# Modulation computed tile by tile, with the first four in-projections behind it; memory keys and values moved to the second mixer

## The chip, the core and the metric

The kernel runs as one program on one NeuronCore of a Trainium2 chip. The metric is the device time of one execution in microseconds. The program uses five instruction streams: TensorE (PE) for matrix products, VectorE (DVE) and ScalarE (ACT) for elementwise work, GpSimd (POOL) for a few clears and products, and SyncE (SP), whose stream issues every DMA. Each stream runs in its own order; semaphores link them.

## The reference, cut to what matters

One block of a two-mixer network on a batch of 1, 512 tokens of width 1024, in float32. The first mixer is attention beside a convolution, both fed by one modulated norm; the second is an RWKV-style recurrence beside an attention over 256 memory tokens; then a feed-forward layer.

```python
mod = jax.nn.silu(c) @ w_mod[l] + b_mod[l]              # shift, scale, gate: 1024 each
shift, scale, gate = jnp.split(mod, 3, axis=-1)
mod_c = jax.nn.silu(c_ctx) @ w_mod[l] + b_mod[l]        # the same for the context
u = rms_norm(h, norm_w[l]) * (1.0 + scale[:, None, :]) + shift[:, None, :]
uc = rms_norm(hc, norm_w[l]) * (1.0 + scale_c) + shift_c
p = u @ w_in[l]                                         # q, k, v, gates, GLU inputs a and g
k_c, v_c = kv_heads(uc @ w_in[l][:, K_LO:V_HI], k_norm_w[l])
...
u = a * jax.nn.sigmoid(g)                               # then a depthwise convolution, 31 taps
out = jnp.concatenate([attn, conv], axis=-1) @ w_out[l]
h = h + gate[:, None, :] * out
...
log_w = -jax.nn.softplus(-(w0 + jnp.tanh(wd) @ w2)) - 0.5   # low-rank products, rank 64
a = jax.nn.sigmoid(a0 + ad @ a2)
```

The second mixer also norms the 256 memory tokens, multiplies them by a key matrix and a value matrix (1024 to 256 each), and attends to them.

## The kernel before

Activations are feature-major: a tensor of width 1024 is 8 tiles of 128 partitions by 512 tokens. Weights come as blocks of 128 x 1024 values (512 KB), in the order of the list `BLOCKS`, into a ring of 6 slots. The SP stream issues them in that order; a block waits until the last user of its slot is through.

**Split products.** Each large product is made of three passes over float32r parts: `weights_high` (ACT, L1351) copies a block to its high part, `weights_low` (DVE, L1697) makes the low part, the activations have the same two parts, and PE runs three matmuls per tile (L698, L699, L700), 24 per block. Two buffers of high and low weights alternate.

**Front of the program.** SP loads the memory tokens, tables, the small vector table, the context, two key blocks, 8 `shift` and 8 `scale` blocks with the residual `xT` between them, two value blocks, then the in-projection blocks. PE sums the squares of memory and context (L675), makes the memory keys (L685) and their head sums, then the modulation (L727). A modulation block there is 128 rows of the matrix by 1024 columns, so shift and scale are complete only when all 16 blocks are in. PE turns the two rows into columns (L739) and makes the memory values (L766). Meanwhile DVE and ACT norm the memory and the residual; at the end DVE applies scale and shift to the 8 tiles (L1706), ACT makes the high parts (L1357), DVE the low ones (L1702), and the first in-projection `a0` starts (L698).

**In-projections.** 22 blocks: a0 g0 a1 g1 a2 g2 a3 g3, k, v, q0 to q3, zc0 to zc3, za0 to za3. Between them DVE makes gates and convolution taps (L1622; one tap is one instruction of 128x512). `IN_TAPS` says how many taps stand beside each block: 97 of 124 in all. The other 27 (`LATE_TAPS`) are done in attention, `CONV_STEP` = 4 per step.

**Attention.** 16 steps of two heads. In a step PE makes the scores (L854), turns probabilities (L809) and makes values (L873); DVE takes the row maxima (L1808), divides (L1822, L1825) and does its taps; ACT exponentiates (L1388) and copies turned tiles (L1304). The scores of a step wait until the exponentials of the step ahead have freed their banks. Small extra work of PE (gate modulation, convolution statistics, pointwise products) is set by `BESIDE_ATTENTION`.

**Out-projections and second mixer.** PE makes out0 to out7, then the sum of squares `h1_sum` (L708). ACT and DVE norm the residual, split the 8 tiles, and PE makes `wdad` and `gd`, then k_0, the low-rank products w and A of pair 0 (`low_rank`, L708), r_0, v_0, sums, the low-rank products of pair 1, k_1 and r_1. Then 6 pairs of heads follow: for each, an inverse is built in levels 2, 4, 8, 16, 32 (L1006, L1019, L1022, at the last level L1032), solved (L1055), and chained over chunks (L1066 to L1098). `low_rank(p + 2)` stands after the solve of pair p and before a part of the next k projection, whose PSUM bank is the one of w. ACT's exponentials of w and A (L1271) stand behind its two copies of the solution. After the pairs come the mixing and the feed-forward products (from about 750 us on), which the change does not touch.

## Time and profile before

| what | value |
|---|---|
| median of 3 runs | 1159.25 us (1155.62 to 1159.65) |
| the profiled execution, device time | 1152.58 us |
| its span | 1150.8 us |
| TensorE clock granted, mean share of full | 0.987 |
| busy over the span | PE 1070.5 us, DVE 660.6, ACT 431.9, POOL 12.0 |
| moved by DMA | 94.93 MB |

The profile comes from one execution, 6.7 us below the median of the runs. Its span is 1.8 us shorter than its device time. An engine's idle time counts only where another engine waits for it, so the stages are read one by one.

### The profile page before, as it was taken

To read this page: it belongs to the slowest core of one execution; us is meant where nothing else is said; L and a number is where in the kernel's file an instruction comes from. 1 tells how busy PE (TensorE), PEld (TensorE's weight loads), DVE (VectorE), ACT (ScalarE), POOL (GpSimd) and SP (SyncE) were. 2 spreads that over 40 slices of the span, in tenths; PEclk is the share of its full clock that TensorE was granted. 3 is DMA by queue.
4 is the path that set the end of the run, shared out by engine and by line. 5 is a ranking of instruction groups with operands and counts; after the bars stand their busy time and mean duration, and the time that the engine had idled before them with its cause. 6 is when DMAs were issued, how large, how long until landed. Compare 5 with 4: busy or idle time off the path is not lost.

```text
span 1150.8 us, 21841 instructions
## 1 busy us (share of the span) xinstructions
PE 1070.5 (93%) x9476; PEld 820.4 (71%) x9476; DVE 660.6 (57%) x1035; ACT 431.9 (38%) x701; POOL 12.0 (1%) x13
## 2 busy tenths in 40 slices
PE   6799999788997888999998989999999999999998
PEld 4377877465575667777676766678888888888887
DVE  2578899987355576667675826565444222444232
ACT  3333354557533642424333313444443211344121
POOL 0000000000000000000000000000000000000000
PEclk9999999999998989999999999999999999999999
DMA  8841322400032120010110004023222333232330
GB/s 345 319 130 60 104 73 73 148 1 1 19 120 82 51 79 21 21 39 21 39 39 21 21 2 185 3 77 107 92 92 93 109 92 102 87 104 92 110 101 28
DMA packets 25581, 94.93 MB, mean 82 GB/s; under 512 B 2832, under 2 KB 2832, under 8 KB 24976
## 3 DMA queue, kind: packets, MB, share of 16 engines
q1 hardware_dynamic: 25488, 93.54, 24.5%
q8 instruction: 76, 1.25, 0.4%
q14 instruction: 17, 0.14, 0.0%
HBM read 89.34 MB, written 4.19 MB: 81 GB/s over the span
## 4 chain that ended last, share of the span: by engine, by line
PE 57%; DVE 4%; ACT 2%; issue 1%; ACTq 0%; DVEq 0%
PE psum L698 14%; PE psum L699 14%; PE psum L700 14%; PE psum L708 4%; PE psum L1006 2%; PE psum L1019 1%; PE psum L1055 1%; PE psum L974 1%; PE psum L1022 1%; PE psum L1098 1%; PE psum L1089 1%; DVE work L2098 1%; PE psum L996 1%; PE psum L1078 1%; PE psum L928 1%
## 5 line engine op out<-in xcount | busy, mean ns | idle before, releaser
L1697 DVE TENSOR_TENSOR weights_low<-ring,weights_high 128x1024 fp32r<-128x1024 f32 x72 | 88.3, 1226 | 75.0 <-ACT weights_high L1351 75.0
L1351 ACT ACTIVATE weights_high<-ring 128x1024 fp32r<-128x1024 f32 x72 | 75.7, 1052 | 127.5 <-PE psum L700 127.5
L1304 ACT ACTIVATE work<-psum 128x384 f32<-128x384 f32 (+2 forms) x125 | 58.5, 515 | 113.0 <-PE psum L1055 48.9
L698 PE MATMUL psum<-normed_high,weights_high 128*128 128x512 f32 x256 | 100.2, 391 | 0.2 <-DVE weights_low L1697 0.2
L700 PE MATMUL psum<-normed_high,weights_low 128*128 128x512 f32 x256 | 99.7, 390 | 0.0
L699 PE MATMUL psum<-normed_low,weights_high 128*128 128x512 f32 x256 | 99.7, 390 | 0.0
L700 PE MATMUL psum<-hidden_high,weights_low 128*128 128x512 f32 x256 | 99.7, 389 | 0.0
L698 PE MATMUL psum<-hidden_high,weights_high 128*128 128x512 f32 x256 | 99.7, 389 | 0.0
L699 PE MATMUL psum<-hidden_low,weights_high 128*128 128x512 f32 x256 | 99.7, 389 | 0.0
L698 PE MATMUL psum<-pair_normed_high,pair_weights_high 128*128 128x512 f32 x176 | 77.2, 439 | 12.2 <-DVE normed_low L1702 4.2
L1622 DVE SCALAR_TENSOR_TENSOR work<-work,small_sb 128x512 f32<-128x512 f32 x116 | 80.1, 745 | 0.0
L698 PE MATMUL psum<-normed_high,in_weights_high 128*128 128x512 f32 x176 | 70.7, 402 | 2.6 <-DVE in_weights_low L1697 2.6
L699 PE MATMUL psum<-normed_low,pair_weights_high 128*128 128x512 f32 x176 | 70.5, 400 | 0.0
L700 PE MATMUL psum<-pair_normed_high,pair_weights_low 128*128 128x512 f32 x176 | 70.1, 398 | 0.0
L700 PE MATMUL psum<-normed_high,in_weights_low 128*128 128x512 f32 x176 | 68.7, 390 | 0.0
L699 PE MATMUL psum<-normed_low,in_weights_high 128*128 128x512 f32 x176 | 68.5, 389 | 0.0
L1601 ACT ACTIVATE work<-work 128x512 f32<-128x512 f32 x32 | 20.2, 632 | 100.9 <-DVE work L1619 100.9
L698 PEld LDWEIGHTS psum<-normed_high,weights_high 128*128 128x128 f32 x256 | 48.1, 188 | 10.9 <-issue 0.9
L698 PEld LDWEIGHTS psum<-pair_normed_high,pair_weights_high 128*128 128x128 f32 x176 | 33.8, 192 | 30.7 <-issue 10.6
L699 PEld LDWEIGHTS psum<-normed_low,weights_high 128*128 128x128 f32 x256 | 48.1, 188 | 10.1 <-issue 0.2
L698 PEld LDWEIGHTS psum<-hidden_high,weights_high 128*128 128x128 f32 x256 | 48.1, 188 | 10.0
L700 PEld LDWEIGHTS psum<-hidden_high,weights_low 128*128 128x128 f32 x256 | 48.1, 188 | 10.0
(239 smaller groups left out, 2059.0 us busy)
## 6 DMA issues: line engine op xcount, KB each, us to landing
ring<-weights SPq DMA_DIRECT2D x154, 512.0 KB, 3.6
residual<-xT SPq DMA_DIRECT2D x1, 2048.0 KB, 18.6
residual_saved<-residual SPq DMA_DIRECT2D x8, 256.0 KB, 2.0
residual<-residual_saved SPq DMA_DIRECT2D x1, 2048.0 KB, 9.0
outT<-residual SPq DMA_DIRECT2D x8, 256.0 KB, 3.2
work<-memT SPq DMA_DIRECT2D x1, 1024.0 KB, 5.0
work<-ctxT SPq DMA_DIRECT2D x1, 1024.0 KB, 9.9
small_sb<-small SPq DMA_DIRECT2D x1, 907.0 KB, 7.9
```

Source lines behind the costliest of these rows:

```text
L698: pe.matmul(out, wh, high(k), start=first and n == 0, stop=False)
L699: pe.matmul(out, wh, low(k), start=False, stop=False)
L700: ins = pe.matmul(out, wl, high(k), start=False, stop=last and n == len(order) - 1)
L708: full_inc(pe.matmul(take(name, w), stationary, moving, start=True, stop=True), name)
L928: last = pe.matmul(outs["mo"][h * DH:(h + 1) * DH, qt * P:(qt + 1) * P], VMEM[:, t, (2 * j + h) * DH:(2 * j + h + 1) * DH], MPT[:, v % 2, ...
L974: last = pe.transpose(out[:, c, :], src[:, 2 * c:2 * c + 2, :], tab("ident"))
L1006: ins = pe.matmul(out[rows(q), c, :], NT[rows(1 - q), h, c, :], XN[rows(1 - q), h, c, :], start=True, stop=True)
L1304: free_inc(act.activation(out, bank(name, w) if src is None else src, ACT.Copy), name)
L1351: act.activation(WH[group(q)][:, q % 2, :], ring[:, SLOT[b], :], ACT.Copy).then_inc(w_high, 1)
L1601: act.activation(FS[:, t, :], FS[:, t, :], ACT.Square).then_inc(h_relu, 1)
L1622: return vec.scalar_tensor_tensor(out=out, in0=a, scalar=scalar, in1=b, op0=op, op1=ALU.add)
L1697: vec.tensor_tensor(WL[group(q)][:, q % 2, :], ring[:, SLOT[b], :], WH[group(q)][:, q % 2, :].bitcast(F32), ALU.subtract).then_inc(w_low, 1)
```

## The change

It moves work and does not remove any product.

- A shift or scale block is now 128 columns of the matrix with all 1024 rows, so that one block of each gives one tile of 128 features. PE makes a tile `m{k}` with 16 small matmuls of 128 columns (32 records in a trace), on four column groups in turn (`modulated`), ACT copies it, PE turns it (4 columns), and DVE, ACT, DVE make tile k of the residual: product by scale and rstd, high part with the shift as bias, low part.
- Four in-projections (`EARLY` = a0, g0, a1, g1) advance tile by tile in the same loop, each in its own PSUM bank; six weight buffers take the place of two for the first six blocks.
- Nine more places for blocks (15 slots in all) hold the first blocks; residual tiles come first, in four pieces, then two modulation blocks and an in-projection block in turn.
- The context is loaded, summed (at tile 5) and modulated later; its shift is added by ACT.
- The memory's load, norm, keys and values move to the out-projections and to the start of the second mixer. The low-rank weights load later.
- `IN_TAPS` of the first 8 blocks sum to 21 where they were 31; `CONV_STEP` is 5, so 37 taps stand in attention. The convolution's mean is one step later.
- `low_rank(p + 2)` stands before the last level's update, and ACT's two exponentials (`pair_start`) before its copies of the solution.

```diff
-CONV_STEP = 4
+CONV_STEP = 5
-IN_TAPS = [0] + [4, 5] * 3 + [4] + [8, 9, 6, 4, 4, 4, 3] + [4] * 5 + [5, 3]
+IN_TAPS = [0, 2, 0, 3, 4, 3, 5, 4] + [8, 9, 6, 4, 4, 4, 3] + [4] * 5 + [5, 3]
...
+EARLY = ("a0", "g0", "a1", "g1")
+EARLY_BEFORE = {"a0": 0, "g0": 1, "a1": 2, "g1": 3}
+BLOCKS = ([n for k in range(DK)
+           for n in [f"shift{k}", f"scale{k}"] + [x for x in EARLY if EARLY_BEFORE[x] == k]]
+          + IN_BLOCKS[len(EARLY):] + [f"gate{k}" for k in range(DK)] + ["pw0", "pw1"]
...
+EARLY_BLOCKS, EARLY_ROOMS = 2 * DK + len(EARLY), 9
+OWN_BUFFERS = 6
+CTX_TILE = 5
... sync
-            sp.dma_start(MEM, memT).then_inc(mem_in, 16)
-            sp.dma_start(CTX, ctxT).then_inc(ctx_in, 16)
+            for j in range(DK // 2):
+                sp.dma_start(X[:, 2 * j:2 * j + 2, :], xT[:, 2 * j:2 * j + 2, :]).then_inc(x_pair_in[j], 16)
+                if name == "out6":
+                    sp.wait_ge(*is_free(f"pw{CK - 1}"))
+                    sp.wait_ge(*is_free(f"o{NQ - 1}"))
+                    sp.dma_start(MEM, memT).then_inc(mem_in, 16)
+                    sp.wait_ge(out_low, DK)
+                    for i in range(len(MEMORY_BLOCKS)):
+                        sp.dma_start(MEMW[:, i, :], weights[len(BLOCKS) + i]).then_inc(memory_weights_in, 16)
... tensor
+                for kk in range(DK):
+                    for half, wt in enumerate(wts):
+                        group_at = (2 * half + kk % 2) * GROUP_COLS
+                        ins = pe.matmul(out[group_at:group_at + GROUP_COLS, :], SILU_C[:, kk, :],
+                                        wt[:, kk * P:(kk + 1) * P], start=kk < 2, stop=kk >= DK - 2)
+            for k in range(DK):
+                first, second = early_parts(k)
+                pe.wait_ge(u_low, k + 1)
+                early_products(k, first)
+                modulated(k + 2)
+                early_products(k, second)
+                modulated_turn(k + 2)
+                if k == CTX_TILE:
+                    pe.wait_ge(squares, DK // 2 + 1)
+                    sum_over("ctx_sum", lambda k: CTXSQ[:, k, :], DK, SC)
...
+            memory_keys(0, 0, DK // 2)
+            pe.wait_ge(tiles_summed, 1)
             one("h1_sum", tab("ones"), SQ1[:, 0, :])
+            memory_keys(0, DK // 2, DK)
+            memory_keys(1, 0, DK // 2)
...
+            memory_values(0, 5)
             project_part("v_0", 0, DK)
...
             project_part("r_1", 0, DK)
+            memory_values(5, MT * DK)
...
+                    if b == LEVELS[-1] and p + 2 < NP:
+                        low_rank(p + 2)
... scalar
+            for k in range(DK):
+                act.wait_ge(x_scaled, k + 1)
+                act.activation(UH[:, k, :], U[:, k, :], ACT.Identity, bias=MOD[:, 0, k, 0:1]).then_inc(u_high, 1)
+                if k < len(EARLY) - 1:
+                    weights_high(k + 1)
+                modulated_rows(k + 2)
+                if k == CTX_TILE - 1:
+                    act.wait_ge(ctx_in, 16)
+                    act.activation(CTXSQ, CTX, ACT.Square).then_inc(squares, 1)
+                if k == CTX_TILE:
+                    rms("ctx_sum", RS[:, 1, 0:SC], SC, 1.0 / D, EPS, rstd)
... vector
+            for k in range(DK):
+                modulated_columns(k)
+                scaled_product(U[:, k, :], X[:, k, :], MOD[:, 1, k, 0:1], RS[:, 0, :]).then_inc(x_scaled, 1)
+                if k < len(EARLY):
+                    weights_low(k)
+                if k == DK - 1:
+                    context_scaled(0, 2)
+                vec.wait_ge(u_high, k + 1)
+                vec.scalar_tensor_tensor(out=UL[:, k, :], in0=U[:, k, :], scalar=MOD[:, 0, k, 0:1],
+                                         in1=UH[:, k, :].bitcast(F32), op0=ALU.add, op1=ALU.subtract).then_inc(u_low, 1)
```

PE's stream at the front of the program, before:

```order
1 L675 MATMUL psum<-work,tables_sb 128x256 x16
2 L685 MATMUL psum<-work,ring 128x256 x16
3 L708 MATMUL psum<-head_squares,tables_sb 128x256 x2
4 L727 MATMUL psum<-ring,silu_cols 32x512 x16
5 L708 MATMUL psum<-work,tables_sb 128x512
6 L727 MATMUL psum<-ring,silu_cols 32x512 x16
7 L739 MATMUL psum<-tables_sb,t_t_61 128x4 x4
8 L739 MATMUL psum<-tables_sb,work 128x4 x4
9 L766 MATMUL psum<-ring,work 128x256 x16
10 L698 MATMUL psum<-normed_high,in_weights_high 128x512
```

and now (L822 is the modulation, L777 its turn, L767 to L769 the three passes of a split product):

```order
1 L744 MATMUL psum<-work,tables_sb 128x512 x4
2 L822 MATMUL psum<-work,silu_cols 32x128 x16
3 L777 MATMUL psum<-tables_sb,t_t_61 128x4
4 L822 MATMUL psum<-work,silu_cols 32x128 x16
5 L777 MATMUL psum<-tables_sb,t_t_61 128x4
6 L767 MATMUL psum<-normed_high,in_weights_high 128x512
```

The first pass of a0 stands behind two modulation tiles, where it stood behind all of the modulation and the memory's products.

ACT's stream now, in the tile loop from tile 4 on (L1428 copies a modulation tile, L1474 makes the high part of a tile, L1480 squares the context, L1380 and L1382 make its rstd; before, the eight high parts stood in one row):

```order
21 L1428 ACTIVATE t_t_61<-psum 128x128
22 L1474 ACTIVATE normed_high<-normed,mod_cols 128x512
23 L1428 ACTIVATE t_t_61<-psum 128x128
24 L1480 ACTIVATE work<-work 128x2048
25 L1474 ACTIVATE normed_high<-normed,mod_cols 128x512
26 L1428 ACTIVATE t_t_61<-psum 128x128
27 L1380 ACTIVATE rstd<-psum 128x256
28 L1382 ACTIVATE rstd<-rstd 128x256
29 L1474 ACTIVATE normed_high<-normed,mod_cols 128x512 x2
```

The high part of tile 5 stands behind the squares of the context, and that of tile 6 behind the context's rstd, which waits for PE.

PE's stream at the end of a pair (pair 1), before:

```order
L1006 MATMUL psum<-work 64x64 x16
L1032 MATMUL psum<-work 64x64 x16
L1055 MATMUL psum<-work 64x128 x16
L708 MATMUL psum<-work,small_sb 128x512 x2
L698 MATMUL psum<-pair_normed_high,pair_weights_high 128x512
```

and now:

```order
L1127 MATMUL psum<-work 64x64 x16
L777 MATMUL psum<-work,small_sb 128x512 x2
L1153 MATMUL psum<-work 64x64 x16
L1176 MATMUL psum<-work 64x128 x16
L767 MATMUL psum<-pair_normed_high,pair_weights_high 128x512
```

The two low-rank products stand ahead of the last update and the solve, no longer between the solve and the projection.

## Rows read from the trace of the kernel before

**Rows 1.** Page, section 1: busy time, share of the span, instructions of each engine.

```profile
PE 1070.5 (93%) x9476; PEld 820.4 (71%) x9476; DVE 660.6 (57%) x1035; ACT 431.9 (38%) x701; POOL 12.0 (1%) x13
```

**Rows 2.** Windows: length, busy us of each engine, then granted clock, DMA share, GB/s.

```profile
0.00:25.00 25.00, 15.87 (x64) 13.15 (x65) 7.12 (x23) 7.40 (x11) 2.36 (x6) 1.00 0.93 374
25.00:50.00 25.00, 17.70 (x82) 4.19 (x80) 10.72 (x17) 8.45 (x17) 0.00 (x0) 0.93 0.88 330
60.00:110.00 50.00, 49.53 (x219) 41.09 (x220) 40.38 (x62) 17.51 (x24) 0.00 (x0) 1.00 0.31 101
110.00:198.00 88.00, 87.18 (x385) 69.11 (x383) 77.59 (x114) 38.38 (x59) 0.00 (x0) 1.00 0.26 84
198.00:242.00 44.00, 33.94 (x268) 20.27 (x266) 41.88 (x69) 24.49 (x54) 0.00 (x0) 0.96 0.29 96
242.00:283.00 41.00, 36.76 (x310) 24.22 (x310) 28.60 (x50) 28.48 (x60) 0.00 (x0) 1.00 0.01 1
```

**Rows 3.** Timeline of PE at the front: start, duration, instruction, idle and releaser.

```profile
50.71 7.15 PE L766 MATMUL psum<-ring,work 128*128 128x256 f32 x32
...
60.47 0.47 PE L698 MATMUL psum<-normed_high,in_weights_high 128*128 128x512 f32 x1 [2.61 <-DVE in_weights_low L1697]
```

**Rows 4.** Timeline: the first load's arrival; modulation blocks as they land.

```profile
5.77 1.91 ACT L1308 ACTIVATE work<-work 128x2048 f32<-128x2048 f32 x1 [3.76 <-DMA work<-memT]
...
46.11 0.19 PEld L727 LDWEIGHTS psum<-ring,silu_cols 128*32 128x32 f32 x4 [1.15 <-DMA ring<-weights]
47.39 0.19 PEld L727 LDWEIGHTS psum<-ring,silu_cols 128*32 128x32 f32 x4 [1.09 <-DMA ring<-weights]
```

**Rows 5.** Timeline of ACT and DVE: squares, split parts of a tile, low weights.

```profile
12.01 1.91 ACT L1310 ACTIVATE work<-work 128x2048 f32<-128x2048 f32 x1 [4.33 <-DMA work<-ctxT]
...
55.22 0.68 DVE L1702 TENSOR_TENSOR normed_low<-normed,normed_high 128x512 fp32r<-128x512 f32 x1
55.33 0.63 ACT L1357 ACTIVATE normed_high<-normed 128x512 fp32r<-128x512 f32 x1 [0.70 <-DVE normed L1706]
```

**Rows 6.** Timeline of PE: matmuls of several shapes at full clock.

```profile
109.54 3.62 PE L685 MATMUL psum<-work,ring 128*128 128x256 f32 x16
...
121.71 3.73 PE L789 MATMUL psum<-ring,work 128*128 128x128 f32 x32
...
218.55 1.53 PE L873 MATMUL psum<-work 128*64 128x128 f32 x24
...
220.81 1.06 PE L727 MATMUL psum<-ring,silu_cols 128*32 128x512 f32 x8
221.89 1.56 PE L854 MATMUL psum<-work 64*128 64x512 f32 x8
```

**Rows 7.** Timeline of DVE in attention: taps of a step, row maxima.

```profile
216.24 2.73 DVE L1622 SCALAR_TENSOR_TENSOR work<-work,small_sb 128x512 f32<-128x512 f32 x4
218.89 1.82 DVE L1808 TENSOR_REDUCE small_temps<-psum 128x1 f32<-128x768 f32 x2
...
247.90 1.82 DVE L1808 TENSOR_REDUCE small_temps<-psum 128x1 f32<-128x768 f32 x2 [2.65 <-PE psum L854]
```

**Rows 8.** Timeline of PE and DVE from the out-projections to pair 0.

```profile
365.70 1.89 PE L708 MATMUL psum<-work,tables_sb 128*128 128x512 f32 x2 [2.24 <-DVE work L1642]
...
400.51 0.47 PE L698 MATMUL psum<-pair_normed_high,pair_weights_high 128*128 128x512 f32 x1 [2.37 <-DVE pair_weights_low L1697]
...
424.81 2.07 PE L708 MATMUL psum<-head_squares,tables_sb 128*128 128x512 f32 x2 [4.69 <-ACT head_squares L1506]
...
419.17 0.43 DVE L1629 TENSOR_SCALAR sigmoids<-sigmoids 128x512 f32<-128x512 f32 x1 [1.94 <-ACT sigmoids L1271]
```

**Rows 9.** Timeline of PE at the end of pair 1.

```profile
505.64 1.15 PE L1032 MATMUL psum<-work 64*64 64x64 f32 x32 [0.75 <-DVE work L2063]
506.94 1.97 PE L1055 MATMUL psum<-work 64*64 64x128 f32 x32 [0.15 <-issue]
508.83 1.13 PE L708 MATMUL psum<-work,small_sb 64*128 64x512 f32 x4
510.81 0.50 PE L698 MATMUL psum<-pair_normed_high,pair_weights_high 128*128 128x512 f32 x1 [0.85 <-ACT sigmoids L1271]
```

396 lines of the change are left out of this document (237 added, 159 removed).

## The prediction

> **What bounds the kernel now.** I read the busy line first: PE is busy for 93% of the span [rows 1], so a gain must come from stretches in which PE waits, or from a better overlap of them. The windows show where these are [rows 2]. In the first 50 us PE is busy 33.6 us while the DMA engines run at 93% and 88%: the front waits for loads. From 60 to 198 us PE has next to no idle time. From 198 to 242 us DVE is busy 41.9 of 44 us and PE 33.9: attention is bound by DVE there. From 242 to 283 us DVE falls to 28.6 of 41 us. Later, PE waits in single gaps: before h1_sum, v_0 and the key sum of pair 1 [rows 8], and at the end of a pair [rows 9].
>
> The front ends when a0 starts, at 60.47 us; nine in-projection blocks later it is 109.54 us [rows 3, 6], so a block takes 5.45 us and g1, the fourth, is through at 60.47 + 21.8 = 82.3 us. The first point of comparison is when g1 is through in the changed kernel.
>
> **The front.** Loads: a block of 512 KB lands every 1.28 us [rows 4]. The first load, two blocks long, was there at 5.77 us [rows 4], so a load that ends after n blocks lands at 3.2 + 1.28 n us. Now the residual is first (4 blocks, and 0.4 for the two small tables): it is there at 8.8 us. The modulation pairs, with the in-projection blocks between them, land at 11.4, 15.2, 19.0, 22.8, 26.7, 29.2, 34.3 (behind the context) and 36.9 us.
>
> PE's work per tile: an m tile is 32 records of 128 columns. Modulation matmuls of 512 columns ran four at a time, 8 in 1.06 us [rows 6], which is 0.033 us for each 128 columns; 24 records of 128 columns on two column groups took 1.53 us, 0.064 each; 32 on the whole array took 3.73 us, 0.117 each [rows 6]. I take 1.0 us for a tile, near the first since the column groups are used alike; the ends are 0.9 and 3.7 us. The turn takes 0.3 us with its waits. A tile of one in-projection is 5.45/8 = 0.68 us. All tile products together are 4 x 5.45 = 21.8 us, as before.
>
> The first tiles go at the pace of a chain: residual in, squares and pair sums (1.0 + 0.7), the sum on PE (two low-clock matmuls took 1.89 us [rows 8], so about 12.5 us for its end), rstd 1.3, m0 and its copy and turn, product 0.7, high part 0.63, low part 0.68 [rows 5]. ACT handles the row copy of tile k+2 ahead of the high part of tile k+1, so tiles 0, 1, 2 are ready at about 18, 22 and 25 us. From tile 2 on PE is full. Tile 2: 1.36 + 1.0 + 2.05 + 0.3 = 4.7 us, until 30. Tile 3: 2.05 + 1.0 + 2.7 + 0.3 = 6.1, until 36. Tiles 4 and 5: 2.05 + 1.0 + 0.7 + 0.3 = 4.05 each. Two waits come in that the order shows: the high part of tile 5 stands behind the row copy and the context's squares (1.91 us, [rows 5]), which costs PE 2.6 us; the high part of tile 6 stands behind the context's rstd, which waits for ctx_sum (8 matmuls, 3.62 us, [rows 6]), 2.2 us more. Then 36 + 4.05 + 2.6 + 4.05 + 3.6 + 2.2 + 2 x 2.7 = 57.9 us. For the clock I add 1.0: it stood at 0.93 of full from 25 to 50 us in the trace of before [rows 2], and the new front has PE idle in pieces as well. **g1 is through at 59 us, 23.3 us earlier.** With m at 3.7 us it would be about 72; with no stall at all 53.
>
> What hides the rest: the memory's products were 3.62 x 2 (keys) and 7.15 us (values, [rows 3]) in the front; they are now later and are priced there.
>
> An m tile switches PE between a four-group and a whole-array form. The trace shows the switch: after 8 four-group matmuls the next one starts when they have ended, at 221.89 for 221.87 us [rows 6], while two forms on the whole array elsewhere overlap by some 0.17 us. The Trainium skill ("TensorEngine Tiling (Array Packing)", Key Properties) says that changing the tiling mode drains TensorE; by that rule 12 switches in the loop from tile 2 on cost some 2 us, estimated from that overlap, and the trace agrees. The 1.0 us of a tile has room for it.
>
> **In-projections after g1.** PE's 18 blocks and the small products took 82.3 to 198.2 us, 116 us, nearly without idle time [rows 2]. DVE's own work in the same stretch now: 87 taps at 0.67 us (four take 2.73 with their overlap, [rows 7]) = 58 us, 16 weights_low at 1.15 = 18, 24 gate operations of 0.4 to 0.6 = 12, rotary 14, waits for rstd and ACT 6: 108 us, under 116. One place is late: the first gates, taps and the context's shift all come after g1, and ACT copies the weights of a3 only after eight context tiles. I put 1 us on PE there. So attention starts 22.3 us earlier.
>
> **Attention.** Each of the seven first steps gets a fifth tap, 0.665 us, in a stretch where DVE is the bound. Late taps go from 27 to 37: 6.7 us of DVE. DVE had a wait of 2.65 us in step 8 [rows 7], which takes the last of them, so 4 to 5 us are left. The later mean only moves 1.88 us of PE from step 7 to step 9, and both statistics steps of the variance into one. **+4.5 us**, ends 0 (PE catches up in the PE-bound steps) and +6.7.
>
> **Second mixer up to pair 0.** Memory adds PE work: keys 7.2, values 7.2, mem_sum and head sums 1.5 us, together 16 us. Its cover: the gaps of 2.24 us, of the norm (wdad is paced by DVE there, about 1.3 us a tile against 0.68 us of PE), of 2.37 and of 4.69 us [rows 8]. Key products in the first gap and between the tiles of wdad fit; h1_sum no longer runs at 1.2 GHz, as it did after 2.24 us of idle time (1.89 us for two records that take 1.13 elsewhere). Until r_0 the two kernels are level. memory_values(0, 5) takes 2.3 us in a gap of 2.37, the other eleven 5.0 us in one of 4.69. ACT's early exponentials (pair_start) save the two waits of DVE for them (one of 1.94 us, [rows 8]) and bring pair 1's inputs forward by about 2 us; and with no gap the key sum takes 1.1 us and not 2.07. **-2.6 us.** Ends: -5 (all of the low clock comes back) and +3 (values delay the key sum and DVE does not gain).
>
> If the cover were gone, the 16 us would stand on the path. SP waits for o3 and pw3, then for all low parts of the gated tiles, before it loads out6: memory (2 blocks) and four blocks land by about 332 us on the old axis, out6 one block after, 15 us before its use. mem_norm on DVE delays out6's addition by about 1 us beside PE's out7: nothing.
>
> **Pairs.** In pairs 1 to 3 PE waits 0.75 us before the last update (for DVE's masks), then 0.85 us before the projection, for the bank that ACT frees by its exponential of w, 1.1 us of it behind the low-rank products [rows 9]. The low-rank products (about 1.0 us) move into the first gap, so the update is 0.3 us later, and the projection follows the solve at once: 0.96 - 0.3 + 0.85, about 1.5 us each; in pair 0, without the first gap, 1.0. Pairs 4 and 5 have none. **-5.5 us**, ends -6.5 and 0 (the solve is the longer chain through DVE and ACT, and copies come later).
>
> **Sum.** -22.3 + 4.5 - 2.6 - 5.5 = -25.9. From the profiled execution, 1152.6, this gives 1126.7; the runs' median is 6.7 us above that execution, and from 1159.25 it gives 1133.3. I forecast **1133 us**.
>
> **Rivals.**
> 1. *The small modulation matmuls do not overlap.* At 0.064 to 0.117 us a record a tile takes 2.0 to 3.7 us, and PE is the bound in the loop: g1 at 64 to 72. For it: half of the records I have for 128 columns run so. Against: the same column groups at 512 columns ran four at a time. Sum: 1138 to 1147. Chance 0.2.
> 2. *The load order gives all, but DVE gives it back.* The first five steps of DVE's in-projection loop start late, taps run behind to the end and attention's steps take the whole 6.7 us, and the values stand in the path: 1133 + 3 (taps) + 2 + 3 = 1141. For it: only 8 us of slack in 116. Chance 0.12.
> 3. *It goes better.* No stall at the context's squares or rstd, attention absorbs half of the taps, the pairs give 6.5: 1133 - 5 - 2 - 3 = 1123, or a little less. Chance 0.1.
> 4. *Slower than before.* The clock gate: small matmuls and waits leave PE at 1.2 GHz through the whole tile loop. PE's 33 us of work between 18 and 58 us then take 66, g1 is through at about 91, 9 us later than before, and with +4.5 - 2.6 - 5.5 the time is about 1165 (less than 6 us over). It decides from some 17 us of loop work at half clock on, at which the front gains only the 6 us that attention takes. Against: before, PE was busy only 17.7 of 25 us from 25 to 50 and the mean clock was 0.93. Chance 0.03.
> 5. *It doesn't do what it says.* Loads issued without waits share the engines and the first residual pieces come late, near 30 us; the loop then starts 12 us later: 1145. Against: in the trace of before, ten loads were on the way and the first was in at 5.8 us. Chance 0.05.
>
> **How the numbers follow.** The forecast's own band, 1126 to 1140, has 0.5. The range of 1120 to 1147 holds it, rivals 1 and 2 and most of 3 and 5. Within 0.5% (5.8 us, about what a measurement of this kernel can tell from no change) would need 20 us of the 26 to be lost: 0.04; slower by more than that 0.04; faster 0.92.
>
> **What would show it.** In the changed profile: the first split product near 18 us; g1's gate exponential near 59; PE gaps of about 2 us at tiles 5 and 6; modulation groups of 32 records in 1.0 us; attention steps of 6.3 us at first, where they were 5.6; no gap over 1 us before v_0 and the key sum of pair 1, and a clock of 1.0 there; no wait for the exponential of w in the pairs. If the records of L822 stand 0.1 us apart, or DVE is over 95% busy from 60 to 175 us, the sum is wrong.

## The result

The changed kernel took 1145.83 us (median of 4 runs, 1142.65 to 1147.52), the kernel before beside it 1159.45 us (1155.62 to 1163.23). The ratio is 0.9888, 95% interval 0.9865 to 0.9912: **faster by 1.1%, 13 us**. In a second comparison, on the chip of the first experiments, the ratio was 0.9861 (0.9838 to 0.9885): 1140.56 for 1158.05 us. The forecast was 1133 us, 26 us below; the measured time lies in its range, but the gain is half to two thirds of what was forecast.

### The profile page after: what moved, and what is told of

Same layout as the page of the kernel before. It is cut to its first block, busy times and chain, and to the rows that moved or that the text cites. A ratio compares the mean times of both kernels' runs of the same rounds, so it can differ in the third digit from the quotient of the medians.

```text
span 1142.5 us, 22265 instructions
## 1 busy us (share of the span) xinstructions
PE 1071.6 (94%) x9660; PEld 825.2 (72%) x9660; DVE 658.2 (58%) x1032; ACT 435.6 (38%) x711; POOL 12.1 (1%) x13
## 3 DMA queue, kind: packets, MB, share of 16 engines
q1 hardware_dynamic: 26064, 93.54, 24.2%
## 4 chain that ended last, share of the span: by engine, by line
PE 81%; DVE 10%; ACT 4%; issue 3%; DMA 1%; SPq 0%; ACTq 0%; DVEq 0%
PE psum L767 20%; PE psum L768 19%; PE psum L769 19%; PE psum L777 5%; PE psum L1127 3%; PE psum L927 2%; DVE work L1773 2%; DVE small_temps L1952 1%; PE psum L898 1%; PE psum L943 1%; PE psum L1140 1%; PE psum L1176 1%; PE psum L1095 1%; PE psum L1199 1%; DMA work<-weights 1%
## 5 line engine op out<-in xcount | busy, mean ns | idle before, releaser
L1458 ACT ACTIVATE weights_high<-ring 128x1024 fp32r<-128x1024 f32 x72 | 75.7, 1052 | 127.5 <-PE psum L769 127.5
L767 PE MATMUL psum<-normed_high,weights_high 128*128 128x512 f32 x256 | 100.1, 391 | 0.2 <-DVE weights_low L1829 0.2
L769 PE MATMUL psum<-normed_high,weights_low 128*128 128x512 f32 x256 | 99.6, 389 | 0.0
L767 PE MATMUL psum<-hidden_high,weights_high 128*128 128x512 f32 x256 | 99.6, 389 | 0.0
L769 PE MATMUL psum<-hidden_high,weights_low 128*128 128x512 f32 x256 | 99.6, 389 | 0.0
L1428 ACT ACTIVATE work<-psum 128x384 f32<-128x384 f32 (+2 forms) x124 | 58.1, 514 | 72.3 <-PE psum L898 29.9
L767 PE MATMUL psum<-pair_normed_high,pair_weights_high 128*128 128x512 f32 x176 | 77.0, 438 | 3.0 <-DVE work L1770 2.2
L769 PE MATMUL psum<-pair_normed_high,pair_weights_low 128*128 128x512 f32 x176 | 69.4, 394 | 0.0
L767 PE MATMUL psum<-normed_high,in_weights_high 128*128 128x512 f32 x144 | 60.1, 417 | 7.9 <-DVE normed_low L1859 6.9
L769 PE MATMUL psum<-normed_high,in_weights_low 128*128 128x512 f32 x144 | 57.1, 397 | 0.0
L768 PE MATMUL psum<-normed_low,in_weights_high 128*128 128x512 f32 x144 | 56.9, 395 | 0.0
L767 PEld LDWEIGHTS psum<-normed_high,weights_high 128*128 128x128 f32 x256 | 48.0, 188 | 10.9 <-issue 0.9
L767 PEld LDWEIGHTS psum<-hidden_high,weights_high 128*128 128x128 f32 x256 | 48.0, 188 | 10.1
L769 PEld LDWEIGHTS psum<-normed_high,weights_low 128*128 128x128 f32 x256 | 48.0, 188 | 10.0
L769 PEld LDWEIGHTS psum<-hidden_high,weights_low 128*128 128x128 f32 x256 | 48.0, 188 | 10.0
```

Of the source, the lines that this page charges most:

```text
L767: pe.matmul(out, wh, high(k), start=first and n == 0, stop=False)
L768: pe.matmul(out, wh, low(k), start=False, stop=False)
L769: ins = pe.matmul(out, wl, high(k), start=False, stop=last and n == len(order) - 1)
L1428: free_inc(act.activation(out, bank(name, w) if src is None else src, ACT.Copy), name)
L1458: act.activation(wsplit(q)[0], room_of(b), ACT.Copy).then_inc(w_high, 1)
```

## Profile after

The busy line answers to [rows 1]: the busy times of PE and DVE are the same within 3 us, so the gain is idle time of PE that went.

```profile
PE 1071.6 (94%) x9660; PEld 825.2 (72%) x9660; DVE 658.2 (58%) x1032; ACT 435.6 (38%) x711; POOL 12.1 (1%) x13
```

The windows answer to [rows 2] (length, busy us, granted clock, DMA share, GB/s). The changed kernel is about 14 us ahead in the third and fourth, so they hold other work than before.

```profile
0.00:25.00 25.00, 12.58 (x113) 7.04 (x113) 9.00 (x21) 11.31 (x18) 0.51 (x5) 0.89 0.93 351
25.00:50.00 25.00, 21.47 (x195) 16.20 (x196) 10.67 (x22) 7.15 (x11) 0.00 (x0) 0.91 1.01 409
60.00:110.00 50.00, 46.95 (x210) 37.76 (x210) 40.91 (x63) 23.35 (x38) 0.92 (x1) 1.00 0.17 53
110.00:198.00 88.00, 83.19 (x355) 61.67 (x353) 76.29 (x112) 36.89 (x57) 0.00 (x0) 0.94 0.28 90
198.00:242.00 44.00, 34.61 (x300) 23.49 (x302) 43.69 (x72) 24.60 (x56) 0.00 (x0) 0.96 0.22 73
242.00:283.00 41.00, 34.92 (x287) 22.70 (x284) 29.60 (x53) 29.75 (x63) 0.00 (x0) 1.00 0.00 1
```

The front is still full of loads (0.93 and 1.01 of the DMA engines), the clock is at 0.89 and 0.91 there, and from 198 to 242 us DVE has 0.3 us of idle time: attention's first steps are bound by DVE more than before.

PE's timeline, with idle time and releaser in brackets, in answer to [rows 3, 8, 9]:

```profile
14.09 1.08 PE L822 MATMUL psum<-work,silu_cols 128*32 128x128 f32 x32
...
17.37 1.08 PE L822 MATMUL psum<-work,silu_cols 128*32 128x128 f32 x32 [1.31 <-DMA work<-weights]
...
20.29 0.80 PE L767 MATMUL psum<-normed_high,in_weights_high 128*128 128x512 f32 x1 [1.01 <-DVE normed_low L1859]
...
25.74 0.79 PE L767 MATMUL psum<-normed_high,in_weights_high 128*128 128x512 f32 x1 [0.81 <-DVE normed_low L1859]
...
31.19 0.50 PE L767 MATMUL psum<-normed_high,in_weights_high 128*128 128x512 f32 x1
...
49.50 0.50 PE L767 MATMUL psum<-normed_high,in_weights_high 128*128 128x512 f32 x1 [2.71 <-DVE normed_low L1859]
...
61.27 0.50 PE L767 MATMUL psum<-normed_high,in_weights_high 128*128 128x512 f32 x1 [2.32 <-DVE normed_low L1859]
...
79.34 0.47 PE L767 MATMUL psum<-normed_high,in_weights_high 128*128 128x512 f32 x1 [1.02 <-DVE in_weights_low L1829]
...
187.73 1.23 PE L943 MATMUL psum<-work 64*128 64x512 f32 x2 [3.29 <-DVE work L1946]
...
423.12 1.10 PE L777 MATMUL psum<-head_squares,tables_sb 128*128 128x512 f32 x2 [0.78 <-ACT memory_keys_values L1428]
...
502.26 1.96 PE L1176 MATMUL psum<-work 64*64 64x128 f32 x32 [0.16 <-issue]
504.16 0.50 PE L767 MATMUL psum<-pair_normed_high,pair_weights_high 128*128 128x512 f32 x1
```

And a step of attention on DVE, in answer to [rows 7]:

```profile
212.58 3.40 DVE L1773 SCALAR_TENSOR_TENSOR work<-work,small_sb 128x512 f32<-128x512 f32 x5
215.90 1.82 DVE L1952 TENSOR_REDUCE small_temps<-psum 128x1 f32<-128x768 f32 x2
217.63 0.16 DVE L1966 RECIPROCAL small_temps<-small_temps 128x2 f32<-128x2 f32 x1
217.82 1.15 DVE L1969 TENSOR_SCALAR normed<-normed,small_temps 128x768 f32<-128x768 f32 x2
218.88 3.40 DVE L1773 SCALAR_TENSOR_TENSOR work<-work,small_sb 128x512 f32<-128x512 f32 x5
```

The first rows are modulation tiles, 32 records in 1.08 us, the second of which waits 1.31 us for its load. Tiles 0, 1 and 2 start at 20.3, 25.7 and 31.2 us. The steps of 5.45 us between them fall into 10.2 us in which PE was granted 1.2 GHz. The gaps at tiles 5 and 6 (2.71 and 2.32) and before a3 (1.02) are those that were forecast. The 3.29 us before the first scores were not. In pair 1 the projection at 504.16 follows the solve at once, where it waited 0.85 us. A step of attention is 6.3 us of DVE (212.58 to 218.88) without idle time.

The points at which the stages end, read in the traces (us). The two middle columns are a second profiled execution of each kernel, from the experiments:

| | before | before_again | after_again | after |
|---|---|---|---|---|
| g1's last product | 82.5 | 84.7 | 66.9 | 67.1 |
| last in-projection | 198.3 | 200.5 | 184.3 | 184.4 |
| out0 starts | 319.7 | 323.2 | 315.0 | 315.2 |
| out7 ends | 363.5 | 368.5 | 360.9 | 361.1 |
| pair 0's first products | 426.8 | 432.8 | 424.0 | 424.1 |
| pair 4's first products | 636.5 | 642.7 | 628.9 | 627.8 |
| last instruction | 1150.8 | 1156.8 | 1143.4 | 1142.5 |

From the first and the last column, stage by stage: front -15.4, in-projections +1.5, attention +9.3, out-projections +2.1, up to pair 0 -0.2, pairs 0 to 3 -6.1, rest +0.5: together -8.3 us. The forecast had -23.3, +1, +4.5, nothing, -2.6 and -5.5. Between the second pair of executions, before_again and after_again, the stages differ by -17.8, +1.6, +8.0, +0.5, -1.1, -5.2 and +0.4, together -13.4 us. So the front and attention are to be explained, and besides why the profiles differ by 8 us and the medians by 13 to 17.

Part of that is which executions were profiled. The experiments below give more executions of the same code in these two stages. In the table (us) "low" is the time in the stage in which PE was granted 1.2 GHz. low_rank_back, no_memory, filled_front and ctx have the changed kernel's attention as it is; low_rank_back and no_memory also its front, and 'banks' both but for the PSUM banks.

| execution | its time, median of its kernel | low up to g1 | g1 through | low in attention | attention to out0 |
|---|---|---|---|---|---|
| before | 1152.6, 1159.3 | 3.4 | 82.5 | 6.8 | 121.4 |
| before_again | 1158.6, 1157.8 | 13.7 | 84.7 | 6.8 | 122.7 |
| after | 1144.3, 1145.8 | 13.6 | 67.1 | 17.1 | 130.7 |
| after_again | 1145.2, 1140.6 | 13.6 | 66.9 | 17.1 | 130.7 |
| low_rank_back | 1153.1, 1142.4 | 10.3 | 65.4 | 10.2 | 127.4 |
| no_memory | 1135.4, 1137.7 | 6.8 | 64.6 | 10.3 | 127.4 |
| filled_front | 1138.7, 1138.4 | 3.4 | 65.7 | 10.2 | 127.5 |
| ctx | 1138.6, 1143.3 | 3.4 | 56.6 | 13.6 | 127.2 |
| banks | 1138.9, 1140.6 | 3.4 | 64.8 | 10.2 | 126.5 |

Two things follow. Where before and changed front had about the same low time, the front gained 17.6 or 17.7 us (84.7 to 67.1 with 13.7 and 13.6; 82.5 to 64.8 with 3.4, by the front of 'banks'), not 15.4. And the two profiles of the changed kernel have more low clock in attention than the others: the same attention code took 127.2 to 127.5 us four times. A stage that is compared with after_again, whose profiled run is the longest of its six, looks better by about 2 us in the front and 3 us in attention by the clock alone.

## Experiments

All medians, with the ratio to the kernel before and its interval:

| kernel | median us | ratio | 95% interval |
|---|---|---|---|
| after_again | 1140.56 | 0.9861 | 0.9838 to 0.9885 |
| banks | 1140.63 | 0.9853 | 0.9829 to 0.9877 |
| taps | 1142.88 | 0.9879 | 0.9857 to 0.9900 |
| ctx | 1143.25 | 0.9880 | 0.9851 to 0.9909 |
| early_split | 1141.45 | 0.9861 | 0.9838 to 0.9883 |
| low_rank_back | 1142.40 | 0.9882 | 0.9849 to 0.9915 |
| no_memory | 1137.72 | 0.9836 | 0.9811 to 0.9861 |
| filled_front | 1138.40 | 0.9835 | 0.9813 to 0.9857 |
| reordered | 1133.40 | 0.9784 | 0.9753 to 0.9815 |
| reordered_filled | 1131.55 | 0.9769 | 0.9747 to 0.9791 |
| reordered_taps | 1129.61 | 0.9757 | 0.9735 to 0.9778 |
| reordered_92 | 1128.25 | 0.9753 | 0.9718 to 0.9788 |
| before_banks | 1159.57 | 1.0019 | 1.0002 to 1.0036 |
| low_rank_on_pe | 1157.82 | 1.0010 | 0.9991 to 1.0030 |
| low_rank_alone | 1153.89 | 0.9973 | 0.9949 to 0.9997 |
| before_again | 1157.82 | 1.0006 | 0.9979 to 1.0033 |

The kernels ran on four chips: after_again, banks, taps and ctx on one; early_split, low_rank_back, no_memory and filled_front on a second; the four from 'reordered' to reordered_taps and before_banks on a third, the rest on a fourth; across chips the ratios compare, not the times. Differences of 1 to 3 us between kernels are within these intervals; for them the stages in the traces are read, but each trace is one execution, and a difference of 1 to 3 us of a stage can be its clock.

### The two kernels again

No edit.

> The changed kernel as it is, run beside the experiments that change one thing in it, so that their differences are read on one chip. Expected: 1143 to 1148 us (1145.8 before), front through g1 at 67.1 us, last in-projection over at 184.4, a 3.3 us gap of PE before the first scores, out0 at 315.

> The kernel before as it is, for a second profiled execution, since the first was faster than its runs' median. Expected of theory E (the executions of one kernel differ only in where PE runs at half clock): span 1150 to 1158 us, the same waits of PE at the same places, and the difference of the spans within 1 us of half of the difference of the times at low clock in which PE is busy.

The cores' rows (span, mean granted clock) of before, before_again, after and after_again:

```profile
core 0: 1150.8 us, clock 0.987
```
```profile
core 0: 1156.8 us, clock 0.981
```
```profile
core 0: 1142.5 us, clock 0.983
```
```profile
core 0: 1143.4 us, clock 0.982
```

The median of after_again, 1140.56 us, is below the 1143 to 1148 us that were expected. The in-projections after g1 take 115.8 us in both executions of before, to 0.01 us. They differ where PE was granted 1.2 GHz: 30.7 us of the first span, 44.4 us of the second. Half of the 13.7 us between them is 6.8, the spans differ by 6.0. So theory E stands in the time, within its 1 us; the waits of PE are nearly the same behind a0, but not in the front, where the second execution has one more wait for a load (1.65 us) and 3.13 us before a0 for 2.61. Of the 11 runs of before beside after_again none was over 0.985; the lowest clock, 0.976, belongs to the longest time, 1161.6, and the two highest, 0.984 and 0.985, to the two shortest, 1153.6 and 1153.9. Of the 64 runs of before beside all experiments three reached 0.988 (1150.6, 1153.8 and 1154.1 us). The first profiled execution, 0.987, was therefore an unusually quick one of this kernel, while the changed kernel's 0.983 lies in the lower half of its own ten runs (0.979 to 0.989). Against before_again the changed kernel's spans are 13.4 and 14.3 us shorter, which is what the medians say.

### Attention: banks, before_banks, taps

**banks** swaps the PSUM banks of the front:

```diff
-            o.append((f"m{k}", 1, 4 + k % 2))
+            o.append((f"m{k}", 1, k % 2))
...
-            o.append((f"mt{k}", 1, 6 + k % 2))
+            o.append((f"mt{k}", 1, 2 + k % 2))
...
-            o.extend((x, 1, EARLY.index(x)) for x in early_parts(k)[late] if EARLY_BEFORE[x] == k)
+            o.extend((x, 1, 4 + EARLY.index(x)) for x in early_parts(k)[late] if EARLY_BEFORE[x] == k)
...
-    o.extend((x, 1, 4 + n) for n, x in enumerate(IN_BLOCKS[len(EARLY):2 * CK]))
+    o.extend((x, 1, n) for n, x in enumerate(IN_BLOCKS[len(EARLY):2 * CK]))
```

> One thing: the PSUM banks of the front are swapped (early projections in banks 4 to 7, the modulation's tiles in 0 to 3), so that the banks that rotate through the in-projections end as they did in the kernel before: za0 to za3 in banks 4 to 7, the first scores' banks 0 to 3 free. Theory B (the bank of za3 holds the first scores back): the gap of 3.3 us before the scores goes, the first scores start within 0.3 us of the end of the last in-projection, PE is not throttled from 186 to 197 us, out0 comes 4 to 6 us earlier and the time is 1140 to 1142. Rival (attention is bound by DVE with its fifth tap, the wait only shows it): DVE's steps run as before, out0 comes less than 1.5 us earlier, and the time is 1144 to 1146.

**before_banks** brings the same assignment of banks into the kernel before:

```diff
-    add("kx", "kc", "hs2", "rot0", "hs3", "vx", "v_lo")
+    o.append(("kx", 1, 0))
+    add("kc", "hs2", "rot0", "hs3", "vx", "v_lo")
```

> The kernel before, with one thing changed: the rotation of the PSUM banks starts four later at the keys, so that za0 to za3 end in banks 0 to 3, where the first scores need them free, as they do in the changed kernel. Theory B: the first scores, which start 0.1 us after the last in-projection in the kernel before, wait for DVE's gate of za3, 3.3 us, the first steps of attention run at the low clock, and attention to out0 takes 124 to 127 us in place of 121.4; time 1160 to 1163 for 1158. Rival (the wait is only a sign of DVE's lag in the changed kernel): a gap of less than 1.5 us, out0 within 1 us of before.

The first scores on PE, in the kernel before and then in before_banks:

```profile
197.91 0.39 PE L700 MATMUL psum<-normed_high,in_weights_low 128*128 128x512 f32 x1
198.23 1.56 PE L854 MATMUL psum<-work 64*128 64x512 f32 x8
```
```profile
201.71 1.22 PE L855 MATMUL psum<-work 64*128 64x512 f32 x2 [3.29 <-DVE work L1803]
```

The same 3.29 us appear to 0.01 us in the other kernel, by nothing but banks. All seven profiled executions with the changed kernel's banks have it, and none of the ten with other banks. From the last in-projection to out0 before_banks takes 124.4 us for 121.4 and 122.7 in the two executions of before, and its ratio is just above 1. In 'banks' the wait is gone, the scores start with the last in-projection's end, and this stage takes 126.5 us. That is 4.2 us less than in after_again, but only 0.9 to 1.0 less than in low_rank_back, no_memory and filled_front, which have the wait and the same 10.2 us of low clock. So theory B holds for the wait; what the wait costs is about 1 us here and 1.7 to 3.0 us in the kernel before, and in the medians 'banks' and after_again are the same. The other 3.3 us of the 4.2 are 6.9 us more of low clock, which varies from 10.2 to 20.5 us between executions that all have the wait. The mechanism: the banks rotate with each small product. The change takes small products out of the front and pins others, so that za0 to za3 ended in banks 0 to 3, where the scores of step 0 need four free banks, and za3's is freed last, by its gate on DVE (L1946), after its sigmoid on ACT. The Trainium skill ("Perfetto Trace Analysis", Matmuls) says that groups should rotate through different banks so that emptying one overlaps the next group's matmuls; the rows agree, and add that a pinned stage behind a rotation needs the rotation to end on the other banks.

**taps** puts the numbers of before into the changed kernel:

```diff
-CONV_STEP = 5
+CONV_STEP = 4
-IN_TAPS = [0, 2, 0, 3, 4, 3, 5, 4] + [8, 9, 6, 4, 4, 4, 3] + [4] * 5 + [5, 3]
+IN_TAPS = [0] + [4, 5] * 3 + [4] + [8, 9, 6, 4, 4, 4, 3] + [4] * 5 + [5, 3]
```

> One thing: the taps as in the kernel before (31 in the first eight blocks, 27 late, four a step). Prediction's theory (taps cost DVE 4.5 us in attention): attention from the last in-projection to out0 gets 4 to 5 us shorter (126 for 130.7), but the 10 taps, 6.7 us, now stand in the in-projections, where DVE had about 8 us of slack: they cost 0 to 3 us there; time 1141 to 1145. Rival (attention's extra 9 us are the bank wait and the low clock, not taps): attention gets less than 1.5 us shorter and the time is 1145 to 1148.

Windows, from g1's end to the last in-projection and from there to out0, of before, after and taps:

```profile
82.50:198.30 115.80, 114.98 (x509) 91.97 (x507) 101.96 (x147) 49.19 (x73) 0.00 (x0) 1.00 0.25 78
198.30:319.70 121.40, 102.56 (x794) 64.28 (x793) 88.00 (x146) 73.09 (x156) 0.00 (x0) 0.97 0.14 44
```
```profile
67.10:184.40 117.30, 115.52 (x507) 91.75 (x505) 101.33 (x148) 52.59 (x82) 0.00 (x0) 1.00 0.25 79
184.40:315.20 130.80, 106.56 (x794) 66.12 (x793) 94.92 (x156) 73.45 (x156) 0.00 (x0) 0.93 0.12 41
```
```profile
65.00:188.50 123.50, 117.07 (x507) 92.86 (x505) 108.32 (x159) 52.34 (x82) 0.00 (x0) 0.97 0.23 76
188.50:313.40 124.90, 107.42 (x792) 66.75 (x792) 88.00 (x146) 73.00 (x156) 0.00 (x0) 0.92 0.13 42
```

Ten taps are 6.9 us of DVE (94.92 - 88.00), as forecast. In 'taps' attention gets 5.8 us shorter and the in-projections 6.2 us longer, where 0 to 3 were expected: a3 waits 5.66 us for its weights, and the low clock follows. The prediction's theory holds for attention; DVE's slack in the in-projections is not where the early taps stand. So the extra 9.3 us of attention are about 5 for taps ('banks' against before, with 3.4 us more of low clock), about 1 for the bank and about 3 for the clock of these two executions; in the four others attention was 5.8 to 6.1 us longer than in the first execution of before.

### The front: ctx, filled_front, early_split, reordered

**ctx** puts the context's squares, sum and rstd behind tile 7:

```diff
-                if name == f"shift{CTX_TILE + 1}":
+                if name == "shift6":
...
-CTX_TILE = 5
+CTX_TILE = DK - 1
...
-                if k == DK - 1:
-                    context_scaled(0, 2)
```

> One thing: the context's squares, its sum and rstd stand after tile 7 and not at tiles 4 and 5 (its load stays where it is). Theory F (ACT's in-order context work makes PE wait at tiles 5 and 6, 2.7 + 2.3 us, and the stall is what drops the clock at 50 us): both gaps go, PE keeps the high clock through 60 us, g1 is through at 60 to 62 us in place of 67.1; ctx_sum stays 1 us behind it, g3 is 3 to 5 us earlier; time 1140 to 1143. Rival (the chain through DVE and ACT paces tiles 4 to 7 anyway): g1 at 65 to 67, time 1144 to 1147.

g1 is through at 56.6 us, 10.3 earlier. Of this 3.6 are the context's sum, which now stands behind g1, and 2.1 are there at tile 2, ahead of both gaps, by the clock; each gap shrank to 0.9 us. But the last in-projection ends at 183.2, only 1.1 earlier, and the median did not fall (1143.25 us, above the expected 1140 to 1143). PE's row behind g1:

```profile
63.30 0.47 PE L767 MATMUL psum<-normed_high,early_high 128*128 128x512 f32 x1 [3.22 <-DVE early_low L1829]
```

PE does the context's sum (3.6 us) and then waits 3.22 us for a2's weights and 1.77 for a3's, which ACT and DVE split behind the context's work; some of the clock is lost with it. Neither expectation had this: the wait that was removed was replaced by one behind it.

**filled_front** adds matmuls without use:

```diff
+            def filler(n):
+                for _ in range(2 * n):
+                    pe.matmul(bank("g1", P), tab("ones"), tab("ones"), start=True, stop=True)
...
                 modulated(k)
+                filler(2 - k)
                 modulated_turn(k)
+                filler(4 - k)
```

and four more behind m2 and its turn each.

> Added: 26 matmuls of 128 columns on the table of ones, into a bank that is overwritten later, in the gaps of PE beside the first three modulation tiles (15 to 25 us). Their results are not used. Theory K (the idle time of PE from 15 to 20 us brings the low granted clock of 19 to 29 us): the clock stays at 1.0 from 16 to 45 us, g1 is through at 63 to 65 us in place of 66.9, time 1138 to 1140. Rival (the first tiles are paced by the chain through DMA, ACT and DVE, so that the clock costs nothing there): g1 moves by less than 1 us, and the filling itself may cost up to 1 us; 1140 to 1142.

These are 28 matmuls (56 records), not 26. Windows of 15 to 30 us in after_again and in filled_front, and the starts of tiles 1 and 2 there:

```profile
15.00:30.00 15.00, 10.39 (x112) 7.21 (x113) 7.95 (x14) 5.70 (x11) 0.00 (x0) 0.66 1.03 417
```
```profile
15.00:30.00 15.00, 14.77 (x205) 12.68 (x195) 8.93 (x17) 7.69 (x13) 0.00 (x0) 1.00 1.03 417
...
25.89 0.48 PE L767 MATMUL psum<-normed_high,in_weights_high 128*128 128x512 f32 x1
...
29.79 0.50 PE L767 MATMUL psum<-normed_high,in_weights_high 128*128 128x512 f32 x1 [0.23 <-DVE normed_low L1870]
```

With PE kept busy the clock stays at 1.00 where it was 0.66; tile 0 starts 1.9 us later, at 22.0, tile 2 1.2 us earlier, g1 at 65.7 for 66.9, where 63 to 65 were expected. A step from tile to tile takes 3.90 us here, with ACT's order unchanged, and 5.45 us in the changed kernel's low stretch; 'taps' and 'ctx', whose low stretch ends at 23.6 us, have 3.91 from tile 1 to 2. The median is 2 us lower, inside the intervals; its clock in four of five runs is 0.991 or more, which no run of after_again and two of six of low_rank_back, on the same chip, reached. Theory K stands for the clock; that the filling is worth time is not shown: with the same front and without it g1 was through at 64.6, 65.0 and 65.4 us in no_memory, 'taps' and low_rank_back.

**early_split** is banks and ctx together, and splits the weights of a2 and g2 inside the loop:

```diff
+                if k in (5, 6):
+                    weights_high(k - 1)
...
-            weights_high(4)
-            weights_high(5)
...
+                if k in (6, 7):
+                    weights_low(k - 2)
...
-            weights_low(4)
-            context_scaled(2, DK)
-            weights_low(5)
+            context_scaled(0, DK)
```

> Three things together: the banks swapped as in 'banks', the context's squares and sum behind tile 7 as in 'ctx', and the weights of a2 and g2 split by ACT and DVE inside the tile loop (tiles 5 to 7) and the context's scaling after them. Theory (behind the loop PE waits for the split weights of a2 and a3, 3.2 and 1.8 us in 'ctx', and nothing else stands between g1 and attention but PE's own 116 us): g1 through at 56 to 59 us, no gap over 1.5 us before a3's products are over, the last in-projection is over at 175 to 178 us (184.4 in the changed kernel, 183.2 in 'ctx'), out0 at 302 to 305, time 1132 to 1135. Rival (DVE bounds the whole of the front and the in-projections, 101 us of work in 117 with the taps in order): the gain comes back as waits at later blocks, last in-projection at 181 to 183, time 1138 to 1141.

A miss: 187.1 us at the last in-projection, later than the changed kernel, and 1141.45 us. PE and ACT:

```profile
79.08 0.77 PE L767 MATMUL psum<-normed_high,in_weights_high 128*128 128x512 f32 x1 [3.54 <-DVE in_weights_low L1829]
```
```profile
73.44 3.29 ACT L1495 ACTIVATE work<-work,mod_cols 128x256 f32<-128x256 f32 x8
76.64 1.99 ACT L1458 ACTIVATE in_weights_high<-ring 128x1024 fp32r<-128x1024 f32 x2
```

a3's high part stands behind the eight context tiles on ACT. PE waits 3.54 us, and runs at the low clock from 78.3 to 85.2 us. It is not DVE's load that gives the gain back (102.9 of 126.2 us), it is one item of ACT's order.

**reordered** mends this one and the first tiles:

```diff
+                if k:
+                    modulated_rows(k + 1)
                 if k < len(EARLY) - 1:
                     weights_high(k + 1)
-                modulated_rows(k + 2)
...
+                    weights_high(6)
                     rms("ctx_sum", RS[:, 1, 0:SC], SC, 1.0 / D, EPS, rstd)
...
-                if x == "g1":
+                if x == "g2":
...
-            context_scaled(0, DK)
+            weights_low(6)
```

(the row copy now stands behind the next tile's high part and ahead of the weights; the context's scaling moves to a2's turn on DVE).

> 'early_split' with two more moves on ACT and DVE: the high part of tile k + 1 stands before the row copy of tile k + 2 on ACT, and a3's weights are split before the context's rstd, its scaling and shift, which follow behind g2's gate. Theory P1 (tile k + 1 waits for the product of tile k and the modulation of tile k + 2 through ACT's order, 5.4 us a tile): tile 1 starts at 23 to 24 us (25.6 before), tile 2 at 27 to 28.5 (31.0), g1 is through at 57 to 59. Theory P2 (a3's weights behind the context's work cost 3.5 us and the low clock that follows them another 3.4): no gap over 1.5 us before a3, no low clock from 70 to 90 us, last in-projection over at 176 to 179 (187.1 in 'early_split', 184.3 in the changed kernel), time 1132 to 1135. Rival (DVE is too full, the waits move to later blocks): 181 to 184 and 1138 to 1141.

ACT's order beside the first tiles, in after and then in reordered:

```profile
18.57 0.28 ACT L1428 ACTIVATE t_t<-psum 128x128 f32<-128x128 f32 x1 [2.00 <-PE psum L822]
18.74 0.71 ACT L1474 ACTIVATE normed_high<-normed,mod_cols 128x512 fp32r<-128x512 f32 x1
19.35 1.04 ACT L1458 ACTIVATE in_weights_high<-memory_keys_values 128x1024 fp32r<-128x1024 f32 x1
24.02 0.28 ACT L1428 ACTIVATE t_t<-psum 128x128 f32<-128x128 f32 x1 [3.62 <-PE psum L822]
24.19 0.71 ACT L1474 ACTIVATE normed_high<-normed,mod_cols 128x512 fp32r<-128x512 f32 x1
```
```profile
18.46 0.71 ACT L1474 ACTIVATE normed_high<-normed,mod_cols 128x512 fp32r<-128x512 f32 x1
19.07 1.04 ACT L1458 ACTIVATE in_weights_high<-memory_keys_values 128x1024 fp32r<-128x1024 f32 x1
21.04 0.72 ACT L1474 ACTIVATE normed_high<-normed,mod_cols 128x512 fp32r<-128x512 f32 x1 [0.93 <-DVE normed L1772]
23.61 0.28 ACT L1428 ACTIVATE t_t<-psum 128x128 f32<-128x128 f32 x1 [1.85 <-PE psum L822]
```

In after tile 1's high part waits 3.62 us behind the row copy of m2, which waits for PE; in reordered it is made at 21.04. Tiles 1 and 2 start at 24.2 and 27.7 us, g1 is through at 54.2, a3 waits 0.61 us, the last in-projection ends at 174.6 and out0 starts at 301.2. Both theories hold, and the median is 7 us below after_again's (ratio 0.9784 for 0.9861). Not all of tile 2's 3.3 us is the order: 'ctx', with ACT's old order and the same 3.4 us of low clock, starts tile 2 at 28.95, and has g1 through at 56.6. So the order is worth 1.2 us at tile 2 and 2.4 at g1. With the clock high throughout (reordered_filled) the step from tile 1 to 2 is 3.51 us for 3.90.

### Slack of DVE: reordered_filled, reordered_taps, reordered_92

These add the filler to 'reordered' (reordered_filled), and then move ten taps (reordered_taps) or five (reordered_92) out of attention:

```diff
-CONV_STEP = 5
-IN_TAPS = [0, 2, 0, 3, 4, 3, 5, 4] + [8, 9, 6, 4, 4, 4, 3] + [4] * 5 + [5, 3]
+CONV_STEP = 4
+IN_TAPS = [0, 2, 0, 2, 3, 4, 5, 5] + [8, 9, 7, 5, 5, 5, 4] + [5] * 5 + [5, 3]
```
```diff
-CONV_STEP = 5
-IN_TAPS = [0, 2, 0, 3, 4, 3, 5, 4] + [8, 9, 6, 4, 4, 4, 3] + [4] * 5 + [5, 3]
+CONV_STEP = 4
+IN_TAPS = [0, 2, 0, 3, 4, 3, 5, 4] + [8, 9, 8, 5, 5, 4, 4] + [4] * 5 + [5, 3]
```

> 'reordered' with the 26 matmuls of 'filled_front' in PE's first gaps. Theory K (the idle time brings the low clock): no low clock before 45 us; the first tiles are up to 1.5 us later by the filling itself, g1 within 1.5 us of 'reordered'; time 0 to 3 us below 'reordered', 1131 to 1134. Rival (the low clock there hides behind the chain): the same time or 1 us more.

> 'reordered_filled' with ten taps moved from attention's first steps (four a step, 27 late) into the in-projections, all of them from g3's block on (33, 40... 97 in place of 87 there). Theory D (DVE has 16 us of slack in the 117 us of the in-projections once a3 is passed, none in attention's first steps): in-projections as long as in 'reordered_filled' within 1 us, attention 4.5 to 6 us shorter (121 to 122.5 in place of 126.5), time 1126 to 1130. Rival (the ten taps cost in the in-projections what they give in attention, as in 'taps', where 6.2 us came for 5.7): the same time as 'reordered_filled' within 2 us.

> 'reordered_filled' with five taps moved from attention into the keys', values' and queries' blocks, four a step, none more in the last eight blocks. In 'reordered_taps' the five more in the last blocks made DVE late for PE at the end of the in-projections (waits of 1.3 us at 149.7 and 4.4 us before the second scores). Theory D2 (these five were the harm): no wait at 149, the scores wait 1.7 us as in 'reordered_filled', attention 122.5 to 124.5 us, out0 at 299 to 301, 1127 to 1129 us. Rival (DVE has no slack for any): as 'reordered_taps', 1129 to 1131.

PE's gaps in reordered_taps, and in reordered_92:

```profile
183.35 1.08 PE L796 MATMUL psum<-ring,silu_cols 128*32 128x512 f32 x4 [4.38 <-DVE work L1959]
```
```profile
149.66 0.47 PE L767 MATMUL psum<-normed_high,in_weights_high 128*128 128x512 f32 x1 [1.16 <-DVE in_weights_low L1842]
...
180.34 0.64 PE L796 MATMUL psum<-ring,silu_cols 128*32 128x512 f32 x4 [1.71 <-DVE work L1959]
```

In reordered_filled the clock is high from 15 us until 180, and g1 is through at 55.7 for 54.2 us; between theory K and its rival the medians, 1131.55 and 1133.40, don't decide. The five more taps in the last blocks made DVE late: 4.38 us before the gate's modulation for 1.71, as D2 says; but the wait at 149.7 us stays with five taps too (1.16 for 1.32), where D2 expected none. In-projections and attention are 120.4 + 127.5 us in reordered_filled, 121.4 + 125.0 in reordered_taps, 121.8 + 124.3 in reordered_92. So moving five to ten taps gives 1.5 to 2 us, not 4.5 to 6, and less if the clock is counted: the trace of reordered_filled has 17.1 us of low clock in attention, those of the other two and of 'reordered' 13.7, and 'reordered', without the move, takes 120.4 + 126.5. The medians fell by 1.9 us (reordered_taps beside reordered_filled, one chip). **reordered_92 is the fastest kernel of this study, 1128.25 us**, 2.5% below the kernel before; between it and the two ahead of it the intervals overlap, and its ratio, 0.9753, is that of reordered_taps, 0.9757.

### Memory and low rank: no_memory, low_rank_back, low_rank_on_pe, low_rank_alone

**no_memory** leaves out products two to seven of every eight of the memory's keys and values:

```diff
                 for k in range(lo, hi):
+                    if 0 < k < DK - 1:
+                        continue
```

> Of the memory's key and value products only the first and last of each group of eight are made, so the memory's keys and values are not computed in full; all else stands. It takes away about 11 us of PE's work between out7 and the key sum of pair 1. Theory (the products lie in waits that are there anyway): r_0 and the key sum of pair 1 come less than 1.5 us earlier and the time is 1139 to 1141. Rival (they stand on the path, and this is why the start of the second mixer gained nothing net): the key sum of pair 1 comes 3 to 8 us earlier and the time is 1133 to 1138.

From wdad's start to gd's end PE takes 15.16 us with them left out and 15.15 with them: key products beside wdad cost nothing. From out0 to pair 0's first products it is 108.2 for 109.0 us, though 2.1 us at low clock fell in it there; the key sum of pair 1 comes 1.7 us earlier. The median is 3 us lower, in the range of the rival, and its interval overlaps that of after_again. So most of the 11 us of products is hidden, as forecast, and about 2 us of it are not.

**low_rank_back** undoes the low-rank part:

```diff
-                    if b == LEVELS[-1] and p + 2 < NP:
-                        low_rank(p + 2)
...
                     solve(p, h)
+                if p + 2 < NP:
+                    low_rank(p + 2)
```

and ACT's `pair_start(p + 2)` stands behind the copies of wu again; **low_rank_on_pe** and **low_rank_alone** bring into the kernel before the reverse edit, on PE alone and on both engines.

> One thing undone: the low-rank products of pair p + 2 and ACT's first exponentials stand behind the solve again. The prediction's theory (1.5 us in each of pairs 1 to 3, 1.0 in pair 0): a pair takes 51.9 us from first level to first level instead of 51.2, the first level of pair 4 stands 4 to 5.5 us later than in the changed kernel, measured from the start of pair 0, and the time is 1144 to 1147 beside 1140.6. Rival (the solve is then late by other waits, the move gives nothing): less than 1.5 us, 1140 to 1142.

> The kernel before with one part of the change alone: the low-rank products of pair p + 2 stand before the last level's update on PE; ACT's exponentials stay where they were. The prediction's theory: the bank wait before the projection stays in part, since ACT reads the banks late; a pair gains 0.5 to 1.0 us in pairs 0 to 3. Rival: the banks' wait was behind ACT all the time, so nothing is gained, or the products delay the update by 1.0 us each: 0 to -0.3 us a pair, pair 0 to pair 4 209 to 211 us (209.7 before).

> The kernel before with the low-rank part of the change whole: the products before the last update on PE, and ACT's first exponentials of pair p + 2 ahead of the copies of wu. The prediction's theory: 1.5 us in each of pairs 1 to 3 and 1.0 in pair 0, pair 0 to pair 4 in 204 us (209.7 before), 1152 to 1153 beside 1157.7. By 'low_rank_back', which lost 2.9 us of the changed kernel's 6.1, it is rather 2.5 to 3.5 us: 206 to 207 and 1154 to 1156, and the rest of the 6.1 is pair 0, which no longer starts at the low clock.

From pair 0's to pair 4's first products: 209.7 us in before, 210.0 in before_again, 211.0 with the move on PE alone, 208.6 with both (206.9 without half of the 3.4 us at low clock that fell in it), 206.3 in low_rank_back, 203.7 and 204.9 (with 3.4 us at low clock) in the changed kernel. The move on PE alone gives nothing: the projection waits 1.27 us for ACT in place of 0.85. With ACT's exponentials the wait goes (its median is 0.3% below before, the interval just under 1), and undoing both costs the changed kernel 1.5 to 2.7 us, between the theory's 4 to 5.5 and the rival's less than 1.5. Its 6.1 us are therefore only in part the low-rank move. Pair 0 is 1.8 us shorter in low_rank_back too (49.98 for 51.82), and there the kernel before starts it at the low clock, behind the 4.69 us gap of [rows 8]. Pair 3 is 2.2 us shorter in it (51.93 for 54.15): two gaps of PE with no releaser are gone, of which the first is, in before and in before_again,

```profile
604.29 0.21 PE L1022 MATMUL psum<-work 64*64 64x64 f32 x1 [1.46 <-issue]
```
```profile
610.21 0.21 PE L1022 MATMUL psum<-work 64*64 64x64 f32 x1 [1.43 <-issue]
```

## Why the prediction was half right

The direction, the stages and most waits were right. The step that failed is the front, -23.3 us forecast and -15.4 measured in the first pair of profiles, -17.6 at equal low clock: the chain of the first tiles with its clock term. Attention's missing term for the bank and the varying clock, and the start of the second mixer, make up the rest.

- **A modulation tile**: 1.0 us forecast, 1.08 measured. Right; rival 1 falls. Where the clock was low, a tile took 1.94 us. At high clock it starts 0.07 us before the modelled end of the product ahead, and the next product 0.07 us before its own end (33.80 for 33.87 us), where products in a row overlap by 0.16; so the 12 switches of form cost about 1 us by the prediction's own measure (an estimate), not some 2.
- **The chain of the first tiles**: tiles 0, 1, 2 at "about 18, 22 and 25 us" were 20.3, 25.7, 31.2. Of the 8.1 us that g1 was late against the forecast of 59, 6.2 are there at tile 2. The first 2.3 are tile 0: the residual's sum ended at 14.2 us, not 12.5, and ACT's copy of m1's row stands ahead of tile 0's high part (18.57, then 18.74 us), with a load that released PE at 17.37 us where 15.2 was forecast. About 0.8 are the period. The prediction names its cause, the row copy of tile k + 2 ahead of the high part of tile k + 1, which closes a loop through PE (product, modulation, copy, high part, low part), and prices it at 3 to 4 us: that is nearly right at the high clock (3.90 in filled_front). The other 3.1 are two turns of this loop at 1.2 GHz (5.45 each).
- **The clock**: +1.0 forecast. From 19.3 to 29.5 and from 50.0 to 53.4 us PE ran at 1.2 GHz. The first stretch cost the 3.1 us, the second 1.5 (from tile 5 to 6 11.77 us, for 10.27 in 'banks', which had no low clock there), so the term was 4.6 us in this execution. In others it was less: g1 was through at 64.6 to 65.7 us. The term was undersized, and it varies. The last 1.5 us of the 8.1 are 0.2 to 0.5 us by which each step from tile 2 on is longer than priced.
- **Tiles 5 and 6**: 2.6 and 2.2 forecast, 2.71 and 2.32 measured. Right in place and size; that removing them brings almost nothing, because of a3's weights and the context's work behind them, was not seen. "No stall at all, 53" would have been true only with ACT's order changed too.
- **In-projections after g1**: +1 forecast, +1.5, with the 1.02 us gap at a3. Right; DVE's work there was 101.3 us, not 108.
- **Attention**: the taps' term, +4.5, was right (+5.1 in 'banks'). Two terms were not in the sum: the bank of the first scores, a wait of 3.29 us worth about 1 us of the stage, and the clock, about 3 us more in the two profiled executions of the changed kernel than in the others. The order and the plan of the banks were there to be read before; the prediction followed engines and loads across the moved instructions, not the banks.
- **Out-projections**: nothing forecast, +2.1. The changed kernel ran 3.5 us of this stage at 1.2 GHz, behind the 2.67 us wait for out0, the first execution of before none. With 3.5 us the stage took 45.9 us, and 45.4 in before_again; with none 44.3 in 'reordered', and 43.8 in before. So about 0.5 us is the kernel's and the rest the clock's.
- **Second mixer**: -2.6 forecast, -0.2. The gaps of 2.37 and 4.69 us [rows 8] went, and ACT's early exponentials did save what was forecast: from DVE's head_rstd of pair 0 to its low weights before pair 1's key sum, 13.4 us for 15.4 (404.60 to 418.01, 407.13 to 422.48). But DVE had waited 1.97 us for PE's head sums before it, 0.96 in before and in no_memory, since the memory's products stand ahead; and the key sum stands behind the memory's values and ACT's copy of them (0.78 us). Counted from out7's end it starts 0.7 us later than in before and runs 1.0 us shorter at the high clock. So the end of +3 that the prediction gives this term ("values delay the key sum and DVE does not gain") came in its first half. And "h1_sum no longer runs at 1.2 GHz" brought nothing since DVE paces wdad (14.7 us for it and gd in before, a third of it at the low clock, 15.15 after, all at the high one). What the clock gave back came in pair 0.
- **Pairs**: -5.5 forecast, -6.1 measured, but by other parts: about 2 to 3 the low-rank move, 2 the clock at pair 0, 2 the two gaps without a releaser.
- **The base**: the sum was put on the median through one profiled execution that was 7 us faster than its kind, and faster by its clock. That did not spoil the forecast, whose terms were differences of work, but in the first two traces alone the gain looks like 8 us where the medians say 13 to 17.
- **Rivals**: 1141 us of rival 2 is near the measured time, but that is luck, not its mechanism: the taps did not run late in the in-projections. Of rival 4 the low clock came for 13.6 us of the front and not the whole loop. The others did not come.

## What to carry to other kernels

When small products are added to or taken from a stage whose PSUM banks rotate, look at which banks the last products before a pinned stage land in, and who frees them last. When a step is moved ahead on an in-order engine, ask whether it waits for an engine that itself waits for what stands behind it; such a loop sets the period, not the sum of durations. Take one stall out together with what is late next: here two stalls of 5 us were worth nothing in the median alone, and 7 us once a3's weights and the first tiles' order went with them. And before a stage is compared between two traces, compare the time that it ran at the low clock: several executions of the same stage here differ by 2 to 3 us by that alone.

## What was not expected of the hardware

- Executions of one kernel differ in how long PE is at 1.2 GHz: 30.7 and 44.4 us in the two of before, with nearly the same waits behind a0. The Trainium skill ("TensorE: Matmul & The Clock Gate", Part 1) says that the slow start varies from run to run, puts its cost under 1% of a typical kernel, and shows a kernel whose long waits bring the low clock back; here it came back up to ten times in a kernel, after shorter waits too, and half of 30.7 to 44.4 us is 1.3 to 1.9% of the span. Ahead of nearly all of these stretches PE had idle pieces of 1 to 5.7 us, and in the front several of 0.5 to 1.3 us in a row.
- Once, in the profiled execution of low_rank_back, PE ran at 1.2 GHz without a break from 727.0 to 750.9 us, busy all the time; ahead of it stood gaps of 0.77 and 1.25 us, which the changed kernel has too, at the same instructions, with its clock at 1.00 over the same window. From pair 4 on this execution took 525.8 us, the two of the changed kernel 514.7 and 514.5; its kernel's median is 1142.4 us, this run took 1153.1. Why the clock did not come back is open.

```profile
727.00:751.00 24.00, 24.00 (x103) 13.64 (x101) 9.83 (x29) 9.78 (x27) 0.00 (x0) 0.50 0.00 0
```

- PE has gaps of 0.8 to 1.9 us inside the pairs for which the traces show no releaser. They stand at the same instruction in two executions of one kernel (1.46 and 1.43 us) and at others in a kernel with other code. Instruction supply would fit that; no run tested it, and it stays open.
